# Expert up weights loaded 16 KB per partition, with the token rows written in a permuted column order

## The chip, the cores and the metric

The kernel runs on one core of one Trainium2 chip. The time is the device time of one execution in microseconds (us). The kernel before takes 1584.23 us, the median of 3 runs (1581.51 to 1584.6).

## What is computed

One layer of a streaming encoder, for 1024 frames of a new stream and 64 frames of a running one; everything is float32. The projection, the two kinds of attention and the output product come first; the change touches the mixture of experts behind them:

```python
x = x + moe(rms_norm(x, g_ffn))          # x: 1088 tokens of 1024 columns

def moe(xf):
    # 4 groups of 8 experts: the best group of each token, in it the best 2 experts
    expert, gate = hier_route(xf)        # g_logits = xf @ w_group, e_logits = xf @ w_erouter
    for each token t and each of its 2 experts e:
        h = silu(xf[t] @ w1[e]) * (xf[t] @ w3[e])    # w1, w3: 1024 x 512
        out[t] += gate * (h @ w2[e])                 # w2: 512 x 1024
```

There are 32 experts. w1, w3 and w2 of one are 2 MB (2048 KB) each.

## The kernel before, in words

The program writes out one instruction stream for each engine, with semaphores between them: SP issues the plain DMAs, GpSimd (POOL) the indirect ones, PE multiplies, DVE and ACT empty its banks. The order is fixed by hand.

**First stages.** SP loads constants, the first rows of x and w_in (1024 rows of 1960 columns, one DMA, L516; each row of 7840 B is one contiguous piece). Nine tiles of projections follow, then the attention stage, which goes over nine tiles of 128 tokens. A hand-written table (`filler`, L147) says which pieces of other work stand between the eight heads of a tile. Among them, for the tile before the current one: `o0` and `o1` (the output product, added to xres), `xnorm` (L1632 to L1634: DVE writes the normed row xn = xres x rs_x x g_ffn), `xna` and `xnb` (eight transposes of 128 columns of xn on PE, L786 to L789), `lg` (router logits, L790 to L796: eight matmuls, chunk k of the transposed row against `w_route[:, k, :]`). SP stores xn to the DRAM tensor `xn_rows` (L586). The pT copies (L495 and L498) and the row maxima (L1661, L1662) of the attention heads stand on DVE too; ACT takes the exponentials (L1159).

`w_route` is loaded once (L544), behind `w_out`, as `(k p) n -> p k n`: partition p gets rows p, 128 + p, 256 + p and so on, eight pieces of 144 B. PE, ACT and DVE wait for six loads on `wout_in` at tile 0 (L868, L1193, L1742): w_out, w_route, chunk_mask, g_mh, g_ffn and state_c.

**Routing.** From about 909 to 944 us DVE works out which token goes to which slot; meanwhile SP loads the weights of expert 0 and w1 of expert 1 (L602, L603), and after the first two gathers have landed w3 and w2 of expert 1.

**The expert stage.** Each expert takes one block of up to 96 tokens. `load_expert` (L470) issues w1, w3 and w2, one DMA each, by `load_part` (L481 to L483), into one of two buffers each. A load of expert e + 2 waits until PE is through with the same matrix of expert e: w1 for h1_full, w3 for h3_full, w2 for y_full. `load_part` has the form `(k p) n -> p k n` for all three: partition p gets rows p, 128 + p, ..., so w1 and w3 arrive as eight pieces of 2 KB per partition (1024 pieces), w2 as four of 4 KB (512 pieces). PE's order per expert b is hidden_1 (the product with w1, L916), the down-projection of b - 1 (L940), the transposes of the token rows of b + 1 (L907), hidden_3 (the product with w3, L916). In `up` (L911), `w[:, k, ...]` meets `x[:, k, :]`, where chunk k of x is the transpose of columns 128 k to 128 k + 127 of the gathered row: row i of the weights must meet column i of the token row.

GpSimd gathers 96 token rows of 4 KB from `xn_rows` for expert b + 2 (L1343), and adds the result rows of expert b to y (L1354, a scatter that waits for the previous one). Its order is gather, then scatter, in a loop; in time the gather of b + 2 follows the scatter of b - 1 (L1362 to L1366). In the records a float32 matmul counts as two instructions. If an expert had more than 96 tokens, further blocks would follow (L961 to L968); in this run none do.

Of the kernel before, what the change touches and what calls it, by code (L numbers as in the profile page):

```python
# [24 lines left out]
ALU = mybir.AluOpType  # L25
# [3 lines left out]
P = 128  # L29
D = 1024  # L30
KD = D // P
# [143 lines left out]
def build(nc, T, O):  # L175

    ctx = ExitStack()
    with ctx:
# [3 lines left out]
        def sem(name):  # L182
            return ctx.enter_context(nc.semaphore(name))
# [74 lines left out]
        w_route = A(KD, NG + NE)  # L258
# [25 lines left out]
        g_ffn = A(D)  # L284
        xres = A(D)
        xn = A(D)
# [25 lines left out]
        def tiny(n, parts=P):  # L312
            a = small[0:parts, sp[0]:sp[0] + n]
            sp[0] += n
            assert sp[0] <= 512
            return a
# [22 lines left out]
        rs_x = tiny(1)  # L339
# [26 lines left out]
        gate_in, mixw_in, wout_in = sem("gate_rows_in"), sem("mix_weights_in"), sem("w_out_in")  # L366
# [29 lines left out]
        x1_sq, x1_rs, xn_ok = sem("res_squares"), sem("res_rstd"), sem("xn_ready")  # L396
# [17 lines left out]
        def wait_full(eng, key):  # L414

            b, k = fills[key]
            eng.wait_ge(full[b], k + 1)
            return bank(RB[b])

        def wait_read(eng, key):  # L420

            b, k = fills[key]
            eng.wait_ge(read[b], k + 1)

        def done_read(ins, key):
            ins.then_inc(read[fills[key][0]], 1)
# [11 lines left out]
        def bc(ap, shape):  # L438
            return ap.unsqueeze(len(ap.shape)).to_broadcast(shape)
# [30 lines left out]
        def load_expert(eng, e, s, signals, done=None):  # L470

            row_up, row_down = ahead(eng, e * D), ahead(eng, e * FF)
            count = None if done is None else ahead(eng, done)
            for row, dst, src, signal, used in ((row_up, w1s[s], "w1", signals[0], h1_full),
                                                (row_up, w3s[s], "w3", signals[1], h3_full),
                                                (row_down, w2s[s], "w2", signals[2], y_full)):
                if done is not None:
                    eng.wait_ge(used, count)
                load_part(eng, row, dst, src, signal)

        def load_part(eng, row, dst, src, signal):  # L481
            rows = T[src].rearrange("e a n -> (e a) n")[bass.ds(row, T[src].shape[1]), :]
            eng.dma_start(dst, rows.rearrange("(k p) n -> p k n", p=P)).then_inc(signal, 16)  # L483

        def gate_col(b):
            return slot_gate[:, bass.ds(b, 1)]
# [21 lines left out]
        def _(sp_):  # L508
# [32 lines left out]
            sp_.dma_start(g_ckv, T["g_ckv"].to_broadcast([P, KL])).then_inc(wuq_in, 16)  # L541
            sp_.dma_start(z_rec, z_dram[0:P, Z_MQ:]).then_inc(zr_in, 16)
            sp_.dma_start(w_out, T["w_out"].rearrange("(k p) n -> p k n", p=P)).then_inc(wout_in, 16)
            sp_.dma_start(w_route, T["w_route"].rearrange("(k p) n -> p k n", p=P)).then_inc(wout_in, 16)  # L544
            for n in range(-1, NT + 1):
                if n >= 1:

# [4 lines left out]
                if n + 1 < NT:  # L552

                    r = slice((n + 1) * P, (n + 2) * P)
                    src = cn[(NC + n + 1) % 2]
# [45 lines left out]
            wait_read(sp_, ("lg", NT - 1))  # L601
            load_expert(sp_, 0, 0, (w1_in[0], w3_in[0], w2_in[0]))  # L602
            load_part(sp_, D, w1s[1], "w1", w1_in[1])  # L603

            for s in range(2):
# [777 lines left out]
        def _(dve):  # L1383
            link = chain(dve, dve_link)
            TT, TS, STT = dve.tensor_tensor, dve.tensor_scalar, dve.scalar_tensor_tensor
# [134 lines left out]
            def fill_work(key):  # L1520
                what, n = key
# [47 lines left out]
                elif what == "qkm":  # L1569
                    o = wait_full(dve, key)  # L1570
                    dve.wait_ge(e_ok, n + 1)
                    done_read(TT(Dm, Dm, o.rearrange("p (a b) -> p a b", b=P), ALU.mult), key)
                elif what in ("ua", "ub"):

                    o = wait_full(dve, key)
                    cur, nxt = state[n % 2], state[(n + 1) % 2]
                    h0 = 0 if what == "ua" else 2
                    if n:
                        wait_read(dve, ("ub", n - 1))
                    if n == 1:  # L1580
                        dve.wait_ge(state_out, 16)

                    mid = cur if n else nxt
                    for h in range(h0, h0 + 2):
                        u = o[:, (h - h0) * CAUG:(h - h0 + 1) * CAUG]
                        dec = decb[0:DK, h * NCH + 2 * n:h * NCH + 2 * n + 1]
                        STT(mid[DK:P, h], cur[0:DK, h], dec, u[0:DK], ALU.mult, ALU.add).then_inc(st1_ok, 1)
                    dve.wait_ge(st1_ok, HM * n + h0 + 2)
                    for h in range(h0, h0 + 2):
                        u = o[:, (h - h0) * CAUG:(h - h0 + 1) * CAUG]  # L1590
                        dec = decb[DK:P, h * NCH + 2 * n + 1:h * NCH + 2 * n + 2]
                        ins = STT(nxt[0:DK, h], cur[DK:P, h], dec, u[DK:P], ALU.mult, ALU.add)
                    done_read(ins, key)
                elif what in ("ia", "ib"):
                    o = wait_full(dve, key)
                    h0 = 0 if what == "ia" else 2
                    view = o[:, 0:2 * CAUG].rearrange("p (a b) -> p a b", b=CAUG)
                    if what == "ia" and n:
                        dve.wait_ge(h_ok, n)
                    done_read(TT(num[:, h0:h0 + 2], view, bc(gt[:, 32 + h0:34 + h0], [P, 2, CAUG]), ALU.mult), key)  # L1600
                    wait_read(dve, key)
                elif what in ("na", "nb"):
                    o = wait_full(dve, key)
                    h0 = 0 if what == "na" else 2
                    view = o[:, 0:2 * CAUG].rearrange("p (a b) -> p a b", b=CAUG)
                    done_read(TT(num[:, h0:h0 + 2], num[:, h0:h0 + 2], view, ALU.add), key)
                    if what == "nb":
                        mlstm_ratio(n)
                elif what == "hsq":
                    dve.wait_ge(hsq_ok, n + 1)  # L1610
                    dve.tensor_reduce(st_m, Dm, AX, ALU.add).then_inc(hs_ok, 1)
                    dve.wait_ge(og_ok, n + 1)
                    link(STT(og, og, 1.0, g_mh, ALU.add, ALU.mult))
                elif what == "hout":

                    dve.wait_ge(hr_ok, n + 1)
                    link(TT(hm, hm, bc(rs_m, [P, HM, DV]), ALU.mult))
                    if n:
                        wait_full(dve, ("mxb", n - 1))
                    STT(mix[:, BANK:], hm.rearrange("p a b -> p (a b)"), 0.5, og, ALU.mult,  # L1620
                        ALU.mult).then_inc(mm_ok, 1)
                elif what == "mxb":
                    o = wait_full(dve, key)
                    if n:
                        wait_full(dve, ("lg", n - 1))
                    done_read(dve.tensor_copy(mixT[:, 4:8], o.rearrange("p (a b) -> p a b", b=P)), key)
                elif what in ("o0", "o1"):
                    o = wait_full(dve, key)
                    dve.wait_ge(xres_in, 16 * (n + 1))
                    lo = 0 if what == "o0" else BANK  # L1630
                    done_read(TT(xres[:, lo:lo + BANK], xres[:, lo:lo + BANK], o, ALU.add), key)
                elif what == "xnorm":  # L1632
                    dve.wait_ge(x1_rs, n + 1)
                    STT(xn, xres, rs_x, g_ffn, ALU.mult, ALU.mult).then_inc(xn_ok, 1)  # L1634
                elif what == "xnb":
                    o = wait_full(dve, key)
                    wait_full(dve, ("o1", n))
                    done_read(dve.tensor_copy(xnT[:, 4:8], o.rearrange("p (a b) -> p a b", b=P)), key)
                elif what == "lg":
                    o = wait_full(dve, key)  # L1640
                    done_read(TT(logits[:, n], o[:, 0:NG + NE], b_route, ALU.add), key)

            def mlstm_ratio(n):

                wait_read(dve, ("na", n))
                wait_read(dve, ("nb", n))
                link(STT(den[:, 0:HM], num[:, :, DV], -1.0, num[:, :, DV], ALU.mult, ALU.max))
                link(TT(den[:, 0:HM], den[:, 0:HM], gt[:, 96:96 + HM], ALU.max))
                link(dve.reciprocal(den[:, HM:], den[:, 0:HM]))
                if n:  # L1650
                    dve.wait_ge(mm_ok, n)
                TT(hm, num[:, :, 0:DV], bc(den[:, HM:], [P, HM, DV]), ALU.mult).then_inc(h_ok, 1)
# [81 lines left out]
            for n in range(-1, NT + 1):  # L1734
# [27 lines left out]
                for key in filler(n, HA):  # L1762
                    fill_work(key)
# [166 lines left out]
```

## Time and profile before

| | before |
|---|---|
| median of 3 runs | 1584.23 us |
| the profiled execution, own time | 1581.9 us |
| its span | 1580.1 us |
| mean granted TensorE clock | 0.947 |
| PE busy | 1438.2 us, 91% |
| DVE, ACT, POOL busy | 483.0, 296.6, 203.8 us |
| DMA | 277.63 MB in 110091 packets, mean 176 GB/s |

PE is TensorE's matmul, PEld its weight load, SPq the queue of SP. The page gives busy shares, then the span in 40 equal slices (39.5 us each), where a 9 is 90% or more. "DMA share" is the mean busy share of the core's 16 DMA engines; overlapping packets can bring it above 1. A packet is one contiguous piece. In brackets behind a group of instructions stands the engine's idle time before it and what released it.

### The profile page before, as it was taken

What the parts mean: (1) busy time and instruction counts of PE and PEld (TensorE: products, weight loads), DVE (VectorE), ACT (ScalarE), POOL (GpSimd) and SP (SyncE); (2) the same over time, 40 slices, a digit from 0 to 9 for tenths busy, and PEclk for the clock granted to TensorE, in tenths of its full rate; (3) what the DMA queues carried; (4) which work ended last, traced back from release to release, by engine and by line L of the source; (5) the groups of instructions that cost most, each with busy time, mean ns of one, the idle gap of its engine ahead of it and who ended that gap; (6) DMA issues with size and microseconds to landing.
All of it is one profiled execution on the core that took longest, in us unless ns stands there. A gap on an engine that the chain in (4) does not pass through costs nothing. (4 is left out here: it accounts for less than half of the span.)

```text
span 1580.1 us, 29898 instructions
## 1 busy us (share of the span) xinstructions
PE 1438.2 (91%) x12716; PEld 985.3 (62%) x12716; DVE 483.0 (31%) x1002; ACT 296.6 (19%) x634; POOL 203.8 (13%) x291
## 2 busy tenths in 40 slices
PE   5899999659998999999999838999999999999996
PEld 2444444236667667768677427777777777777773
DVE  3100100266456557647455461111111111111110
ACT  5201010133323233334332100000000001000000
POOL 3100000022022112101020001111111111111110
PEclk9999999868978999999999859999999999999998
DMA  7021211421011101101101068999999999999992
GB/s 274 14 78 39 77 39 51 145 73 45 24 52 61 68 22 47 68 21 48 60 3 41 27 219 285 356 363 358 362 365 357 363 360 366 370 358 354 361 365 87
DMA packets 110091, 277.63 MB, mean 176 GB/s; under 512 B 8952, under 2 KB 12920, under 8 KB 110028
## 3 DMA queue, kind: packets, MB, share of 16 engines
q1 hardware_dynamic: 102864, 255.33, 44.7%
q0 software_dynamic: 7168, 21.51, 5.4%
q8 instruction: 38, 0.62, 0.2%
q14 instruction: 21, 0.17, 0.0%
HBM read 248.40 MB, written 32.05 MB: 177 GB/s over the span
## 5 line engine op out<-in xcount | busy, mean ns | idle before, releaser
L916 PE MATMUL psum<-arena 128*64 128x96 f32 x8192 | 355.6, 246 | 14.4 <-DMA arena<-in_w 11.6
L916 PEld LDWEIGHTS psum<-arena 128*64 128x64 f32 x8192 | 345.6, 136 | 22.8 <-issue 18.6
L689 PE MATMUL psum<-arena 128*128 128x512 f32 (+1 forms) x576 | 238.1, 574 | 0.6 <-DVE arena L1424 0.6
L940 PE MATMUL psum<-arena 128*96 128x512 f32 x512 | 227.5, 596 | 0.8 <-issue 0.8
L689 PEld LDWEIGHTS psum<-arena 128*128 128x128 f32 x576 | 108.8, 190 | 124.2 <-issue 124.2
L940 PEld LDWEIGHTS psum<-arena 128*96 128x96 f32 x512 | 80.6, 162 | 124.2 <-issue 120.5
L784 PE MATMUL psum<-arena 128*128 128x512 f32 x288 | 130.4, 607 | 0.8 <-issue 0.8
L643 PE MATMUL psum<-ident,arena 128*128 128x128 f32 (+1 forms) x468 | 76.0, 312 | 59.0 <-DVE arena L1518 27.1
L846 PE MATMUL psum<-arena 128*128 128x64 f32 (+3 forms) x848 | 110.1, 274 | 1.5 <-DVE arena L498 0.8
L643 PEld LDWEIGHTS psum<-ident,arena 128*128 128x128 f32 (+1 forms) x468 | 62.2, 155 | 78.8 <-DVE arena L1518 28.8
L846 PEld LDWEIGHTS psum<-arena 128*128 128x128 f32 (+3 forms) x848 | 101.7, 189 | 8.8 <-issue 1.8
L816 PE MATMUL psum<-arena 96*128 96x512 f32 (+4 forms) x224 | 100.1, 561 | 0.4 <-DVE small L1500 0.4
L1159 ACT ACTIVATE arena<-psum,small 64x1104 f32<-64x1104 f32 (+8 forms) x72 | 57.7, 802 | 207.8 <-DVE small L1662 207.8
L784 PEld LDWEIGHTS psum<-arena 128*128 128x128 f32 x288 | 54.4, 194 | 63.6 <-issue 62.4
L1833 DVE COPY arena<-psum 128x768 f32<-128x768 f32 x32 | 30.7, 959 | 203.9 <-PE psum L907 203.9
L1252 POOL TENSOR_SCALAR small<-small 128x2 f32<-128x2 f32 (+4 forms) x44 | 14.4, 328 | 578.6 <-ACT arena L1079 189.8
L1212 ACT ACTIVATE arena<-psum 128x384 f32<-128x384 f32 x32 | 15.7, 492 | 380.4 <-PE psum L916 338.6
L1434 DVE TENSOR_SCALAR arena<-psum,small 128x512 f32<-128x512 f32 x18 | 13.5, 751 | 219.6 <-PE psum L689 219.6
L1218 ACT ACTIVATE arena<-psum,slot_gate 96x1024 f32<-96x1024 f32 x32 | 35.6, 1112 | 217.9 <-PE psum L940 217.9
L1839 DVE SCALAR_TENSOR_TENSOR arena<-arena,psum 128x384 f32<-128x384 f32 x32 | 17.8, 555 | 184.8 <-ACT arena L1212 184.8
L829 PE MATMUL psum<-ident,arena 128*128 128x128 f32 (+3 forms) x424 | 63.0, 288 | 9.6 <-ACT arena L1133 3.8
L1350 POOL COPY now_out<-slot_out 128x1 uint32 (+1 forms) x32 | 5.9, 183 | 478.7 <-ACT arena L1218 478.7
(218 smaller groups left out, 1303.9 us busy)
## 6 DMA issues: line engine op xcount, KB each, us to landing
arena<-in_w SPq DMA_DIRECT2D x96, 2048.0 KB, 20.0
arena<-in_x_rows SPq DMA_DIRECT2D x18, 512.0 KB, 5.2
z_rows<-arena SPq DMA_DIRECT2D x9, 980.0 KB, 4.5
arena<-in_w_in SPq DMA_DIRECT2D x1, 7840.0 KB, 23.2
arena<-z_rows SPq DMA_DIRECT2D x9, 768.0 KB, 5.2
out_y<-arena SPq DMA_DIRECT2D x9, 512.0 KB, 2.6
xn_rows<-arena SPq DMA_DIRECT2D x9, 512.0 KB, 2.9
arena<-in_w_out SPq DMA_DIRECT2D x1, 4096.0 KB, 17.1
```

What stands on the lines that cost most here:

```text
L643: ins = pe.transpose(o[0:width, i * P:i * P + rows], src, ident[0:rows, 0:rows])
L689: ins = pe.matmul(o[:, 0:hi - lo], xT[s][:, k, :], w_in[:, k, lo:hi], start=(k == 0), stop=(k == KD - 1))
L784: ins = pe.matmul(o, mixT[:, k, :], w_out[:, k, lo:lo + BANK], start=(k == 0), stop=(k == KD - 1))
L816: pe.matmul(o[0:q, lo:hi], qT[n % 2][:, h, 0:q], KT[:, h, k0:k0 + hi - lo], start=True, stop=True)
L829: ins = pe.transpose(o[0:w, i * P:i * P + q], probs[0:q, lo:lo + w], ident[0:q, 0:q])
L846: ins = pe.matmul(o, pT[0:w, i, 0:q], v, start=(i == 0), stop=(i == len(blocks) - 1))
L916: ins = pe.matmul(o[c:c + CT, j * EB:(j + 1) * EB], w[:, k, j * P + c:j * P + c + CT], x[:, k, :], start=(k == 0), stop=(k == KD - 1))
L940: ins = pe.matmul(bank(5 + c)[0:EB], hT[:, k * EB:(k + 1) * EB], w2s[s][:, k, c * BANK:(c + 1) * BANK], start=(k == 0), stop=(k == KF - 1))
L1159: act.activation(probs[0:q, 0:w], bank(0, 3)[0:q, 0:w], ACT.Exp, bias=nmax[0:q, h:h + 1], accum_out=rsum[0:q, h:h + 1]).then_inc(s_read, 1)
L1218: act.activation(ye[s][0:EB], bank(5, 2)[0:EB], ACT.Copy, scale=gate_col(col)[0:EB]).then_inc(y_read, 1)
L1833: dve.tensor_copy(xeT[s], bank(0, 2).rearrange("p (k t) -> p k t", t=P)[:, :, 0:EB]).then_inc(xeT_read, 1)
L1839: STT(uu, th, 1.0, bank(2)[:, 0:KF * EB], ALU.add, ALU.mult).then_inc(u_ok, 1)
```

## The change

Three edits. `load_part` takes the form `(p k) n -> p k n` for w1 and w3: partition p gets rows 8 p to 8 p + 7, which adjoin in DRAM, 16 KB. w2 keeps its form. `w_route` gets the same form, 1152 B per partition. With that, chunk k of the weights holds rows k, 8 + k, 16 + k, ...; so the token row must have column 8 q + k at place 128 k + q, and the norm writes it so: its output is viewed with q outside and k, in steps of 128 elements, inside, while xres and g_ffn are read in their own order. xn, `xn_rows`, the transposes and the gathered rows all carry the permuted order; nothing else uses them.

```diff
         def load_part(eng, row, dst, src, signal):
             rows = T[src].rearrange("e a n -> (e a) n")[bass.ds(row, T[src].shape[1]), :]
-            eng.dma_start(dst, rows.rearrange("(k p) n -> p k n", p=P)).then_inc(signal, 16)
+            form = "(k p) n -> p k n" if src == "w2" else "(p k) n -> p k n"
+            eng.dma_start(dst, rows.rearrange(form, p=P)).then_inc(signal, 16)
...
-            sp_.dma_start(w_route, T["w_route"].rearrange("(k p) n -> p k n", p=P)).then_inc(wout_in, 16)
+            sp_.dma_start(w_route, T["w_route"].rearrange("(p k) n -> p k n", p=P)).then_inc(wout_in, 16)
...
                 elif what == "xnorm":
                     dve.wait_ge(x1_rs, n + 1)
-                    STT(xn, xres, rs_x, g_ffn, ALU.mult, ALU.mult).then_inc(xn_ok, 1)
+                    by_row = lambda a: a.rearrange("p (q k) -> p q k", k=KD)
+                    STT(xn.rearrange("p (k q) -> p q k", k=KD), by_row(xres), rs_x, by_row(g_ffn), ALU.mult,
+                        ALU.mult).then_inc(xn_ok, 1)
```

## Rows read from the trace of the kernel before

**Rows 1.** The page: the span in 40 slices.

```profile
DMA  7021211421011101101101068999999999999992
```

**Rows 2.** Table of stages, 10 to 1546 us.

```profile
core 0: us, PE busy (x) PEld busy (x) DVE busy (x) ACT busy (x) POOL busy (x), PEclk, DMA share, GB/s
10.00:25.00 15.00, 10.52 (x34) 4.90 (x32) 5.75 (x13) 9.60 (x25) 6.32 (x7) 1.00 1.01 426
920.00:935.00 15.00, 0.61 (x3) 0.33 (x1) 12.73 (x45) 0.00 (x0) 0.00 (x0) 0.50 1.04 397
960.00:1140.00 180.00, 178.19 (x2761) 136.66 (x2762) 20.69 (x30) 14.89 (x19) 25.50 (x36) 1.00 1.01 352
1141.00:1546.00 405.00, 393.42 (x5883) 295.07 (x5880) 43.45 (x63) 33.70 (x42) 58.08 (x82) 1.00 1.03 362
```

**Rows 3.** Waits of PE, 960 us to the end (us in total, times, longest).

```profile
PE psum L916 <- DMA arena<-in_w: 11.6, 18, 1.1
```

**Rows 4.** Timeline of PE, expert stage: start us, us, what, idle before.

```profile
973.92 7.11 PE L940 MATMUL psum<-arena 128*96 128x512 f32 x16
...
992.45 7.11 PE L940 MATMUL psum<-arena 128*96 128x512 f32 x16
...
1141.10 7.11 PE L940 MATMUL psum<-arena 128*96 128x512 f32 x16
...
1155.21 5.55 PE L916 MATMUL psum<-arena 128*64 128x96 f32 x128 [0.83 <-DMA arena<-in_w]
...
1546.21 7.11 PE L940 MATMUL psum<-arena 128*96 128x512 f32 x16
```

**Rows 5.** DMA, 10 to 25, then 920 to 935, then 1141 to 1546 us.

```profile
DMA packets 815, 6.39 MB, mean 426 GB/s; under 512 B 0, under 2 KB 0, under 8 KB 815
...
DMA packets 2445, 5.96 MB, mean 397 GB/s; under 512 B 48, under 2 KB 48, under 8 KB 2445
...
q0 software_dynamic: 4600, 13.67, 13.2%
```

**Rows 6.** DMA of the whole span: a queue (MB, share), issues (us to landing).

```profile
q8 instruction: 38, 0.62, 0.2%
...
arena<-in_w SPq DMA_DIRECT2D x96, 2048.0 KB, 20.0
...
arena<-in_w_route SPq DMA_DIRECT2D x1, 144.0 KB, 18.5
```

**Rows 7.** Groups of DVE by shape: busy us, mean ns.

```profile
L1634 DVE SCALAR_TENSOR_TENSOR arena<-arena,small 128x1024 f32<-128x1024 f32 x9 | 11.6, 1285 | 2.5 <-POOL small L1254 2.2
...
L1476 DVE TENSOR_TENSOR_SCAN arena<-arena 4x1152 f32<-4x1152 f32 x1 | 2.5, 2545 | 0.0
...
L1477 DVE COPY small<-arena 4x18 f32<-4x18 f32 x1 | 0.2, 165 | 0.0
L1483 DVE COPY small<-small 4x16 f32<-4x16 f32 x1 | 0.2, 163 | 0.0
```

**Rows 8.** Timeline around the norm: the eighth tile, then the last.

```profile
855.43 0.11 DVE L1661 MEMSET psum<- 64x64 f32 x1 [0.16 <-PE psum L818]
...
856.85 1.13 ACT L1159 ACTIVATE arena<-psum,small 128x1040 f32<-128x1040 f32 x1 [2.83 <-DVE small L1662]
...
858.36 0.87 PE L829 MATMUL psum<-ident,arena 128*128 128x128 f32 x6
...
906.50 1.97 PE L643 MATMUL psum<-ident,arena 128*128 128x128 f32 x8 [4.27 <-DVE arena L1634]
```

**Rows 9.** Timeline near 1110 us, then landings of the gather (min/median/max).

```profile
1111.35 10.90 PE L916 MATMUL psum<-arena 128*64 128x96 f32 x256
...
1115.65 1.00 POOL L1343 DMA_INDIRECT arena<-xn_rows,now_tok  x1 [0.83 <-POOL now_tok L1340]
...
1129.13 0.82 PE L907 MATMUL psum<-ident,arena 96*128 96x96 f32 x8
...
DMA to landing us min/median/max: 4.2/8.5/9.9
```

## The prediction

> **What bounds the kernel now.** The page comes first. Its slices show the DMA engines lightly used up to slice 23 and at nine tenths from slice 25 on [rows 1]. That stretch is the expert stage, from about 950 us to the end. The table of stages says both are full there: between 1141 and 1546 us PE works 393.4 of 405 us, the DMA share is 1.03, at 362 GB/s [rows 2]. So I need the row that says which of them yields. The list of waits has one entry in which PE waits for a transfer: L916, the up-projections, on the expert weights, 18 times, 11.6 us [rows 3]. The timeline of PE gives the period. Down-projections (L940) start at 973.92 and 992.45, 18.53 us apart, with nothing idle between; between 1141.10 and 1546.21 lie 21 periods of 19.29 us, and the gaps stand where w1 of the next expert is due [rows 4]. I read it so: PE needs 18.53 us per expert, the DMA engines 19.29. Double buffers give the loads a lead of some experts, which is used up by about 1140 us; from there the loads set the pace. From 973.92 to 1546.21 there are 30 periods: 572.29 us, against 30 x 18.53 = 555.9 us if PE never waited. The difference, 16.4 us, is all that faster loads can give (11.6 us of named waits, the rest late restarts after them). In front of the stage no load of an expert is waited for, and behind it stand one scatter and the end.
>
> **What the change does to the loads.** w1 and w3 of each expert, 64 of the 96 expert loads, go from 1024 pieces of 2 KB to 128 pieces of 16 KB; w2 stays at 512 of 4 KB. Bytes and destination addresses in SBUF are as before. What a piece costs beside its bytes comes from two stretches with nothing else on the DMA engines: 10 to 25 us (w_in, pieces of 7840 B) moved 815 packets, and 920 to 935 us (2 KB and 4 KB pieces) 2445 packets, 48 of them tiny, of 5.96 MB [rows 5]. Per engine that is 15 x 16 / 815 = 0.2945 us for 7840 B and 15 x 16 / 2397 = 0.1001 us for 2486 B on the average. The line through both has 36.3 ns per 1000 B and 9.8 ns per piece. Eight pieces of 2 KB made one save 7 x 9.8 = 69 ns; each engine has 16 such pieces per expert (2 tensors x 128 / 16), so 1.10 us per expert, an estimate that extrapolates from 7840 to 16384 B. The ends: with the rate of the 7840 B pieces alone, 4.19 MB at 426 instead of 397 GB/s [rows 2] save 0.72 us. On the other side the page's instruction queue moved 38 packets of 16 KB in 0.2% of 16 engines' span, or 1.3 us each instead of the 0.60 us of my line [rows 6]; these come singly, each with its way to memory and back, and mine come in a row as w_in's do, so I take 1.10 us and keep that end for a rival.
>
> How much is enough? Without waits the 30 periods need 16.4 us less, and the DMA engines are full from the start of them, so 16.4 / 30 = 0.55 us per expert suffices. 1.10 us is twice that and the 0.72 us still more than that: I expect PE to set the whole stage, and the gain to be 16.4 us, cut off by PE at 18.53 us per expert. What is late next is PE itself; loads will land with a growing lead.
>
> **The token rows.** The norm (L1634) writes element (q, k) to column k x 128 + q, so its output steps 512 B from element to element; it reads as before. The transposes, the gather and the matmuls keep their addresses, so PE's instructions keep number and shape. L1634 takes 1285 ns, nine times. The trace has no strided write of this size. A strided read of 18 elements 256 B apart takes 165 ns beside 163 ns for 16 adjoining ones: nothing to speak of. The slowest row per element is the scan, 2545 ns for 1152, or 2.2 ns each, which would make the norm 2.26 us [rows 7]. I take nothing (nearest row) and keep plus 1.0 us as the other end. What hides it: in the eighth tile the norm stands two copies ahead of the row maximum on DVE; that starts 0.16 us after PE's scores, and the exponential behind it ends near 858.0 where PE takes it up at 858.36. So of 1.0 us more 1.0 - 0.16 - 0.38, some 0.5, would reach PE in each of eight tiles, and all of it in the last tile, where PE's transposes wait for the norm until 906.50: 8 x 0.5 + 1.0 = 5.0 us [rows 8].
>
> The Trainium skill (Advanced Engine Details and Errata, Memory Cachelines) speaks against this write: accesses that each fall into another 16-byte line of SBUF pay a penalty, which it does not price; no row here shows such a write.
>
> **w_route.** One load of 144 KB in 128 pieces instead of 1024. It lands 18.5 us after its issue, behind w_out [rows 6], and PE and the others wait not for it but for six loads, of which state_c is issued last. At most 56 x 9.8 ns = 0.5 us, off the path: nothing. SP's instructions are the same in number.
>
> **The gather.** GpSimd's indirect DMAs share the 16 engines with the loads. The gather issued at 1115.65 lands after 8.5 us (9.9 at most), and the transposes that need it start at 1129.13, 13.5 us after the issue [rows 9]; 5 us are spare. If its rows take turns with the loads' packets, a row now waits behind 0.60 us instead of 0.08. Some ten rows per engine (13.67 MB in 21 periods [rows 5], scatter and gather) make at most 10 x 0.52 = 5.2 us more. Only w3's eight packets per engine lie in the queue at that time, though (its product ends at about 1117, w1's at 1122), so 8 x 0.52 = 4.2 us: just inside. I put its cost at nothing, with a rival.
>
> **The sum.** 1581.9 us of the profiled execution less 16.4 is 1565.5. That execution stands 2.3 us under the median of the runs, 1584.23; I carry the difference over: 1567.8, say 1568.
>
> **The rivals.**
> 1. The loads get faster, but by less than 0.55 us per expert; the gain is 30 x the saving. With 0.36 us, half of the lower end, it is 10.8 us: 1573. For it: fixed costs may overlap while two queues are served. Against: even the rate measured at 7840 B is enough. Chance 0.10. 
> 2. Nothing happens, because the memory gives no more than the 360 GB/s of the expert stage whatever the pieces: 1584. Against it are the 426 GB/s of 10 to 25 us and 397 GB/s of 920 to 935 us [rows 2]; for it, that no row has so large pieces beside gathers. Chance 0.06. The Trainium skill (DMA: Bandwidth & Descriptors, Specifications) puts the memory's limit per core at about 358 GB/s, by which this rival would be the forecast; the trace's 426 does not agree.
> 3. Slower: the gather lands late. Its place is PE's L907, the decision point a landing 13.5 us after issue instead of 8.5. It would take two 16 KB packets ahead of each row instead of one. With a landing at 14.5 us PE waits 1 us in 30 experts: 1568 + 30 = 1598. Chance 0.06.
> 4. Slower: a 16 KB packet costs 1.3 us in a row as well [rows 6]. Then w1 and w3 alone take 16 x 1.3 = 21 us per expert instead of 10.8, and 30 x 10 us are added: about 1880. For it is one rounded row, against it that 7840 B pieces run at 426 GB/s. Chance 0.02.
> 5. The gain comes, but the norm's strided write costs 1.0 us each: 1568 + 5.0 = 1573. Chance 0.12; half of that cost is as likely as all of it.
>
> The forecast itself has 0.64. Together the cases that end under 1581 hold 0.86, rival 2 holds 0.06, the slower ones 0.08. A measurement of this kernel tells about 0.2% (3.2 us) from no change. The range: PE's 18.53 us leaves no room for a larger gain, so only the scatter of runs (3.1 us) lies below: 1564. Above, it takes in rivals 1 and 5 with both costs at part: 1576. Left out are rivals 2 to 4 and some of the tails.
>
> **What would show it.** In the changed profile: about 51,900 DMA packets rather than 110,091 (64 loads x 896 fewer, and 896 for w_route); no PE wait on in_w, or a few below 1 us; L940 every 18.53 us up to the end of the stage; a DMA share in the late stage below the 1.03 of now, and GB/s up from 362 to some 375, since the same bytes pass in less time; in_w landings well under 20 us; L1634 near 1285 ns. I am wrong if L940 stays above 18.6 us with in_w as the releaser (rivals 1, 2, 4), if PE waits at L907 for xn_rows (rival 3), or if L1634 is above 1.5 us and PE idles in the attention stage (rival 5).

## The result, and the profile after

The changed kernel takes 1598.19 us, the median of 20 runs (1582.9 to 1635.33); the kernel before, run beside it, 1584.22 us (20 runs, 1579.4 to 1609.43). The ratio is 1.0067, 95% interval 1.0042 to 1.0092: slower by 0.7%, where 1568 us was forecast. The ratio leaves the disturbed runs out (5 of the 20 of the changed kernel) and is worth 10.6 us; the medians take in all runs and differ by 14.0. The profiled execution took 1590.24 us, with a span of 1588.3.

The table of stages, the waits of PE for transfers in the expert stage, and the DMA of 1141 to 1546 us, of the changed kernel, answer to [rows 2], [rows 3] and [rows 5]:

```profile
core 0: us, PE busy (x) PEld busy (x) DVE busy (x) ACT busy (x) POOL busy (x), PEclk, DMA share, GB/s
10.00:25.00 15.00, 9.77 (x36) 4.72 (x35) 6.45 (x14) 9.60 (x25) 7.19 (x8) 1.00 1.01 426
960.00:1140.00 180.00, 170.35 (x2630) 132.05 (x2632) 19.48 (x28) 13.31 (x17) 23.79 (x34) 0.98 0.95 340
1141.00:1546.00 405.00, 400.44 (x5962) 299.31 (x5962) 44.95 (x65) 34.99 (x44) 59.99 (x86) 1.00 1.01 366
```

```profile
PE psum L908 <- DMA arena<-xn_rows,now_tok: 11.4, 8, 2.6
```

```profile
DMA packets 22033, 148.21 MB, mean 366 GB/s; under 512 B 2286, under 2 KB 2286, under 8 KB 16555
...
arena<-in_w SPq DMA_DIRECT2D x64, 2048.0 KB, 19.9
...
arena<-xn_rows,now_tok POOLq DMA_INDIRECT x21, 13.3
```

No product waits for its weights any more. In their place PE's transposes wait eight times for the gathered token rows, 11.4 us in all, about as much as before in another place: the gather lands a median of 13.3 us after its issue instead of 8.5. The timeline of PE and GpSimd shows one such wait, and the line's landings (min/median/max) answer to [rows 9]:

```profile
996.41 1.01 POOL L1344 DMA_INDIRECT arena<-xn_rows,now_tok  x1 [0.82 <-POOL now_tok L1341]
...
1003.00 7.11 PE L941 MATMUL psum<-arena 128*96 128x512 f32 x16
...
1012.71 0.88 PE L908 MATMUL psum<-ident,arena 96*128 96x96 f32 x8 [2.61 <-DMA arena<-xn_rows,now_tok]
...
DMA to landing us min/median/max: 4.2/13.3/16.3
```

The gather is issued at 996.41, its rows would be wanted at 1010.1, when the down-projection ends, and come at 1012.7.

The other new thing is in front of the expert stage. First the norm by shape [rows 7], then its last place on DVE and the first and last down-projection on PE [rows 8, 4]:

```profile
L1636 DVE SCALAR_TENSOR_TENSOR arena<-arena,small 128x1024 f32<-128x1024 f32 x9 | 17.9, 1993 | 2.5 <-POOL small L1255 2.2
```

```profile
913.52 1.96 DVE L1636 SCALAR_TENSOR_TENSOR arena<-arena,small 128x1024 f32<-128x1024 f32 x1 [2.20 <-POOL small L1255]
...
984.21 7.11 PE L941 MATMUL psum<-arena 128*96 128x512 f32 x16
...
1554.40 7.11 PE L941 MATMUL psum<-arena 128*96 128x512 f32 x16
```

The norm takes 1.99 us instead of 1.28. The span is 8.2 us longer, and this is where: the last norm starts 8.4 us later (913.52 against 905.16); from there to the first down-projection it is 70.7 us instead of 68.8, 1.9 more; the 30 periods take 570.2 us instead of 572.3, 2.1 less; the rest is 33.9 us in both. The profiled execution thus shows 8 us, where the ratio is worth 10.6 and the medians differ by 14.

### The profile page after: what moved, and what is told of

Same layout as the page of the kernel before. It is cut to its first block and busy times, and to the rows that moved or that the text cites. A ratio compares the mean times of both kernels' runs of the same rounds, so it can differ in the third digit from the quotient of the medians.

```text
span 1588.3 us, 29898 instructions
## 1 busy us (share of the span) xinstructions
PE 1443.4 (91%) x12716; PEld 989.6 (62%) x12716; DVE 489.4 (31%) x1002; ACT 296.2 (19%) x634; POOL 203.4 (13%) x291
## 2 busy tenths in 40 slices
DMA packets 51851, 277.63 MB, mean 175 GB/s; under 512 B 7928, under 2 KB 12024, under 8 KB 43596
## 5 line engine op out<-in xcount | busy, mean ns | idle before, releaser
L785 PE MATMUL psum<-arena 128*128 128x512 f32 x288 | 134.0, 621 | 0.8 <-issue 0.8
L1435 DVE TENSOR_SCALAR arena<-psum,small 128x512 f32<-128x512 f32 x18 | 13.5, 751 | 219.2 <-PE psum L690 219.2
```

Of the source, the lines that this page charges most:

```text
L785: ins = pe.matmul(o, mixT[:, k, :], w_out[:, k, lo:lo + BANK], start=(k == 0), stop=(k == KD - 1))
```

## The experiments

Each ran in five rounds beside the kernel before, whose median was 1583.2 to 1587.1 us in these four sessions. The sessions were on three chips, so experiments of different sessions are compared by their ratios to the kernel before. By the way: in the expectations, "568 + the norm's 8" means 1568.

**e1, the loads alone.** Only the edit of `load_part`; the norm and w_route are left in their old order.

> The 16 KB pieces for w1 and w3 alone; the norm writes xn in its own order and w_route keeps its form, so the up-products meet columns in another order than the rows (routing and all sizes are as before). Theory A (the loads gain about 16 us, and the gather of the token rows, landing 13.3 us after issue instead of 8.5, gives most of it back; the strided norm costs some 8 us besides): between 1584 and 1592 us, PE waits on xn_rows of 10 us or more, no wait on in_w, L1634 at 1285 ns. Theory B (the strided norm is the whole loss): 1568 us, gather waits as a side effect gone or below 3 us. Theory C (the DMA engines are still full with 16 KB pieces, the gather waits are only where that shows): as A, with the DMA share at 1.0 or more.

Measured: 1585.57 us, ratio 1.0009 (0.9976 to 1.0043); 8.4 us of waits on xn_rows in 6 places, none on in_w; gather landings 13.0 us. The 30 periods take 569.0 us. So the 16 KB pieces alone gain nothing that these runs can tell (their interval is 0.3% to each side), and the norm is not the whole loss: theory B falls, A or C stands.

**e2, the norm alone.** Only the edits of w_route and of the norm; the loads are left in their old order.

> The permuted norm and w_route alone; w1 and w3 load in 2 KB pieces as before, so the up-products meet columns in another order than the rows (routing and all sizes are as before). Theory A: plus 6 to 9 us, 1590 to 1593, the norm at 1990 ns nine times, the last norm about 6 to 8 us later than before, and the expert stage as before with 11 us of waits on in_w, none on xn_rows. Theory B: plus 20 us or more, 1604. Theory C: as A.

Measured: 1603.42 us, ratio 1.0106 (1.0062 to 1.0149). The expert stage is as before (573.9 us for 30 periods, 13.4 us of waits on in_w), the last norm starts at 926.22. Nearer to B's number than to A's: the norm costs twice what A had for it, 17 us by the ratio. The losses of e1 and e2 add up to 1.15%, more than the 0.67% of the changed kernel, but their intervals (0.6% to 1.7% for the sum) reach down to it.

**e3 and e4, an earlier gather that was none.** I meant to issue the gather one expert earlier, and wrote the loop as scatter of b, then gather of b + 3:

```diff
-                    pool.wait_ge(xeT_full, b + 1)
-                    gather(s, b + 2, xe_in[s])
                     scatter(s, b, ye_out[s], ye_out[1 - s], 16 * (j + s))
+                    pool.wait_ge(xeT_full, b + 2)
+                    gather(1 - s, b + 3, xe_in[1 - s])
```

> The changed kernel whole, with GpSimd issuing the gather of expert b + 3 behind the scatter of b, one expert earlier than now. Theory A: no PE wait on xn_rows and none on in_w, L941 every 18.53 us, 1574 to 1578 us (568 + the norm's 8), the runs closer together than the 50 us they spread now. Theory B: 1594 or more, since the gather was no cause. Theory C: waits on in_w take the place of those on xn_rows, period near 19 us, 1586 to 1592.

> The kernel before with the same earlier gather and nothing else. All theories: the time of before within 2 us, 11 us of waits on in_w as before, since its gathers were never late; if it is faster by 5 us or more, hidden gather waits were part of the time before too, and theory A credits the 16 KB pieces with too much.

Measured: 1600.77 us, ratio 1.007 (1.0023 to 1.0118), and 1586.29 us, ratio 1.0031 (0.9995 to 1.0067). That order is the one the loop had all along, since the gather of b + 2 stands at the head of the next turn, behind the scatter of b - 1. The two are repeats of the changed kernel and of the kernel before, and agree with them.

**e5, the changed kernel with the gather truly earlier.** The buffer of b + 4 is free once the rows of b + 2 are transposed, right behind the down-projection that the scatter of b waits for:

```diff
+            for s in range(2):
+                pool.wait_ge(xeT_full, s + 1)
+                gather(s, 2 + s, xe_in[s])
...
-                    pool.wait_ge(xeT_full, b + 1)
-                    gather(s, b + 2, xe_in[s])
                     scatter(s, b, ye_out[s], ye_out[1 - s], 16 * (j + s))
+                    pool.wait_ge(xeT_full, b + 3)
+                    gather(s, b + 4, xe_in[s])
```

> The changed kernel whole, with the gather of expert b + 4 behind the scatter of b, where the buffer has just come free: truly one expert earlier. (In e3 and e4 it was not: GpSimd's loop already issued the gather of b + 3 behind the scatter of b, so those two repeat the changed kernel and the kernel before.) Theory A (late gathers give back what the loads gain): no wait on xn_rows and none on in_w, L941 every 18.53 us, about 13 us under the changed kernel: 1585. Theory C (the DMA engines are full with 16 KB pieces too): the waits move to in_w, period 19.0 us, time of the changed kernel within 4 us.

Measured: 1584.81 us, ratio 0.9989 (0.9955 to 1.0023). The stage of e5 in the table of stages, cut at 1512 us since its last load is issued at 1525.7 us and has landed by 1541.3, and the landings of its gathers:

```profile
1141.00:1512.00 371.00, 371.00 (x5609) 280.40 (x5607) 41.38 (x60) 32.05 (x40) 56.17 (x79) 1.00 1.01 373
1512.00:1546.00 34.00, 34.00 (x501) 24.83 (x498) 3.18 (x5) 3.20 (x4) 1.79 (x3) 1.00 0.73 281
```

```profile
DMA to landing us min/median/max: 4.1/13.0/16.1
```

The gathers land as late as ever after their issue, but PE works all 405 us and waits for no transfer. The 30 periods take 556.2 us, 18.54 each. A's 13 us are there (12 by the two ratios, 1.0067 and 0.9989). C falls as a cause: the DMA engines are still full while the loads last, with a share of 1.01 at 373 GB/s, but PE doesn't wait for them.

**e6, the loads alone with the earlier gather.** e1 with the loop of e5.

> The 16 KB pieces for w1 and w3 alone (norm and w_route as before, so the up-products meet columns in another order), with the gather of b + 4 behind the scatter of b. e1 without the earlier gather took 1585.6 us, 13 us of it over PE's 18.53 us per expert. Theory A: 1572 us, no waits of PE on transfers in the expert stage. Theory C: 1583 or more, with waits on in_w.

Measured: 1569.48 us (6 runs), ratio 0.9884 (0.9838 to 0.9929). This is the time that was forecast for the change, and what the loads are worth when the gather is early and the norm plain. PE waits for no transfer. The stage of e6, whose last load has landed by 1535.3 us:

```profile
1141.00:1512.00 371.00, 371.00 (x5610) 280.36 (x5608) 41.32 (x60) 32.08 (x40) 55.18 (x78) 1.00 1.01 374
1512.00:1546.00 34.00, 33.24 (x440) 22.92 (x437) 3.18 (x5) 3.21 (x4) 3.21 (x4) 1.00 0.60 221
```

**e7, strided read in place of the strided write.**

```diff
-                    by_row = lambda a: a.rearrange("p (q k) -> p q k", k=KD)
-                    STT(xn.rearrange("p (k q) -> p q k", k=KD), by_row(xres), rs_x, by_row(g_ffn), ALU.mult,
+                    by_row = lambda a: a.rearrange("p (q k) -> p k q", k=KD)
+                    STT(xn.rearrange("p (k q) -> p k q", k=KD), by_row(xres), rs_x, by_row(g_ffn), ALU.mult,
```

> The changed kernel with the same permuted norm, but written in order and read with steps of 32 B. Theory D (the norm's longer write delays PE in the attention stage, and with PE's idle moments comes more time at half clock): if L1636 falls to 1285 ns, the stage ends as before, near 907 us, and the time is that of e1, 1586 us, 12 to 15 under the changed kernel. If strided reads cost the same as strided writes, L1636 stays near 2.0 us and the time at 1598. Rival E (the longer norm is hidden; the spread of the attention stage is chance): 1598 whatever L1636 takes.

Measured: 1595.26 us, ratio 1.0064 (1.0032 to 1.0096). The norm takes 2072 ns: reading in steps of 32 B is no better than writing in steps of 512 B. It doesn't tell D from E.

**e8, e7 with the gather of e5.**

> Both amendments: norm with strided read, gather of b + 4 behind the scatter of b. Theories A and D: 1572 us, faster than both kernels. Theory C: 1585. Theory E: as e5.

Measured: 1587.19 us, ratio 0.9994 (0.9966 to 1.0023), 30 periods 557.7 us, no wait for a transfer. The 1572 us of A and D would have needed a short norm; it takes 2073 ns, and the time is that of e5. The 8 us under e7 (11 by the ratios) are again the gathers.

**e9, the permutation in the transposes.** e6, and in `gather_transposes`:

```diff
-                    ins = pe.transpose(bank(0, 2)[:, k * P:k * P + EB], xe[s][0:EB, k * P:(k + 1) * P],
+                    ins = pe.transpose(bank(0, 2)[:, k * P:k * P + EB], xe[s][0:EB].rearrange("t (q k) -> t k q", k=KD)[:, k, :],
                                        ident[0:EB, 0:EB])
```

> 16 KB pieces for w1 and w3, gather of b + 4 behind the scatter of b, norm and w_route as in the kernel before; the permutation is made by the eight transposes of the gathered rows, which read every eighth column (steps of 32 B). Theory A+D (nothing is lost but by late gathers and the longer norm): if the strided transposes cost PE nothing, 1569.5 us as e6, faster than both kernels. If they take twice their 0.1 us each, 0.8 us in 31 experts: 1594. The row of L908 by shape tells which.

Measured: 1577.29 us, ratio 0.9959 (0.9929 to 0.9989). The transposes of e9, then those of e10 with the plain read, in the groups by shape:

```profile
L908 PE MATMUL psum<-ident,arena 96*128 96x96 f32 x256 | 33.4, 274 | 7.6 <-issue 7.6
```

```profile
L907 PE MATMUL psum<-ident,arena 96*128 96x96 f32 x256 | 27.1, 249 | 7.6 <-issue 7.6
```

A strided read costs PE some 0.2 us per expert; the 30 periods take 563.2 us, 7.0 more than in e5 and e6. Between the two answers expected, nearer to the free one. It beats both kernels, the one before by 0.4%.

**e10, the kernel before with the gather of e5.**

> The kernel before with the gather of b + 4 behind the scatter of b, nothing else: the control for e6 and e9. Theory A: its gathers were never late and its loads still are, so 1584 us with 11 us of waits on in_w, within 2 us of the kernel before. Rival F (the earlier gather alone spreads the transfers better and gives the gain of e6 without 16 KB pieces): 1570, in_w waits below 3 us.

Measured: 1585.41 us, ratio 1.0035 (0.9996 to 1.0073), and this wait of PE:

```profile
PE psum L916 <- DMA arena<-in_w: 12.7, 16, 1.4
```

So the earlier gather gives nothing by itself; F falls.

**e11, a longer norm without a stride.**

```diff
-                    STT(xn, xres, rs_x, g_ffn, ALU.mult, ALU.mult).then_inc(xn_ok, 1)
+                    for at in range(0, D, 147):
+                        part = slice(at, min(at + 147, D))
+                        last = STT(xn[:, part], xres[:, part], rs_x, g_ffn[:, part], ALU.mult, ALU.mult)
+                    last.then_inc(xn_ok, 1)
```

> The kernel before with its norm written in seven plain pieces of 147 columns (the last shorter), no stride anywhere, so that DVE spends some 2.0 us on it instead of 1.28. Theory D (what costs is DVE's time at this place, by delaying PE and by the time at half clock that follows, not the strided access as such): as e2, 1595 to 1603, more than 70 us at half clock between 400 us and the last norm. Rival G (the strided access slows other engines' accesses to SBUF): 1584 to 1588, the attention stage as before.

Measured: 1597.91 us, ratio 1.008 (1.0051 to 1.0108). Its norm in the timeline:

```profile
432.54 2.06 DVE L1636 SCALAR_TENSOR_TENSOR arena<-arena,small 128x147 f32<-128x147 f32 x7
```

The same 2 us of DVE cost 13 us by the ratio without any stride (e2: 17, with intervals that overlap). G falls: beyond its length no cost of the strided access shows. The table of stages over the eight tiles, 430 to 905 us, of the kernel before, e6, the changed kernel, e11 and e2, in this order (the last three columns are the granted clock, the DMA share and GB/s):

```profile
430.00:905.00 475.00, 451.13 (x2421) 327.16 (x2421) 278.12 (x612) 150.12 (x361) 67.84 (x93) 0.95 0.12 42
```

```profile
430.00:905.00 475.00, 452.38 (x2410) 328.22 (x2409) 275.89 (x605) 149.99 (x361) 67.30 (x92) 0.94 0.12 42
```

```profile
430.00:905.00 475.00, 451.39 (x2406) 327.89 (x2405) 282.78 (x610) 148.64 (x359) 67.09 (x91) 0.94 0.12 41
```

```profile
430.00:905.00 475.00, 452.28 (x2396) 332.64 (x2396) 277.37 (x638) 149.01 (x359) 67.11 (x91) 0.92 0.12 41
```

```profile
430.00:905.00 475.00, 452.49 (x2378) 333.88 (x2377) 271.31 (x570) 148.97 (x359) 67.11 (x91) 0.91 0.12 41
```

PE is as busy in all five, some 95% of this stretch, but the granted clock is 0.95 and 0.94 with the short norm and 0.94, 0.92 and 0.91 with the long one (unrounded 0.946, 0.939, 0.935, 0.917 and 0.907). From the first norm to the last it takes 473.0 and 475.8 us with the short norm, 481.9, 489.6 and 496.3 with the long one. Where the clock agrees (e4, which is the kernel before over again, and the changed kernel, both 0.935), it is 475.9 against 481.9 us: 6.0 us, and eight norms are 8 x 0.71 = 5.7 us longer. The remaining 8 to 15 us of e11 and e2 over e6 go with 2 to 3 hundredths of the clock, which over 475 us are 10 to 14 us.

In PE's own records the larger part is not waiting. Between the first and the last norm PE stands idle for 24.0 us in the kernel before, 25.6 in e11 and 26.3 in e2, but is busy for 448.9, 464.0 and 470.0 us: the same products take longer, since more of them run at half clock.

**e12, pieces of 4 KB.** Gather order, norm and w_route of the kernel before, and:

```diff
+            if src == "w2":
+                rows = rows.rearrange("(k p) n -> p k n", p=P)
+            else:
+                rows = rows.rearrange("(a p c) n -> p a (c n)", p=P, c=2)
+                dst = dst.rearrange("p (a c) n -> p a (c n)", c=2)
+            eng.dma_start(dst, rows).then_inc(signal, 16)
...
-xe[s][0:EB, k * P:(k + 1) * P]
+xe[s][0:EB].rearrange("t (a q c) -> t a c q", c=2, q=P)[:, k // 2, k % 2, :]
```

> Pieces of 4 KB for w1 and w3 (two adjoining rows per piece), gather order, norm and w_route as before; the transposes read every second column (steps of 8 B). By the 9.8 ns per piece this saves 0.63 us per expert, just over the 0.55 needed. Theory A (the gather lands late because each of its rows waits behind a 16 KB packet): landing near 9 us, no PE wait on xn_rows, waits on in_w below 3 us, 1569 to 1573 us. Rival H (the gather is late with any faster loads): waits on xn_rows of 5 us or more.

Measured: 1574.56 us, ratio 0.9937 (0.9908 to 0.9966): the lowest of all kernels but e6, which leaves the permutation of the rows out. The profiled execution took 1599.86 us; in it the granted clock is 0.88 between 430 and 905 us, in code that is the same as in the kernel before, but 1.00 in the stretch of the expert stage that is read here:

```profile
1141.00:1546.00 405.00, 405.00 (x6122) 311.11 (x6119) 44.16 (x65) 34.12 (x43) 61.76 (x87) 1.00 1.02 368
```

```profile
arena<-in_w SPq DMA_DIRECT2D x64, 2048.0 KB, 17.8
...
arena<-xn_rows,now_tok POOLq DMA_INDIRECT x22, 8.8
```

```profile
L912 PE MATMUL psum<-ident,arena 96*128 96x96 f32 x256 | 35.0, 281 | 7.5 <-issue 7.5
```

The loads are fast enough for PE never to wait for them, and the gather lands after 8.8 us as with pieces of 2 KB: no wait at all, with the old order of gathers. H falls: it is the 16 KB packets that hold up the gather, not faster loads as such. The periods are 18.8 us, for the transposes are slow here too, at 281 ns each.

**e13, e14 and e15, the norm in two places.** The strided norm is cut in two, half at its place, half at the head of the next slot of the hand-written order:

```diff
-        ... ("ub", n)] * now + [("xnorm", n - 1)] * old,
-        4: [("kn", m), ...
+        ... ("ub", n)] * now + [("xnorm0", n - 1)] * old,
+        4: [("xnorm", n - 1)] * old + [("kn", m), ...
...
+                elif what in ("xnorm0", "xnorm"):
+                    dve.wait_ge(x1_rs, n + 1)
+                    q = slice(0, P // 2) if what == "xnorm0" else slice(P // 2, P)
+                    by_row = lambda a: a.rearrange("p (q k) -> p q k", k=KD)[:, q, :]
+                    ins = STT(xn.rearrange("p (k q) -> p q k", k=KD)[:, q, :], by_row(xres), rs_x, by_row(g_ffn),
+                              ALU.mult, ALU.mult)
+                    if what == "xnorm":
+                        ins.then_inc(xn_ok, 1)
```

e14 does it for the permutation of e12, in four instructions of 256 columns.

> The changed kernel with the gather of b + 4 behind the scatter of b, and its strided norm cut into two halves, one at the norm's place (slot 3 of the hand-written order), one at the head of slot 4, each near 1.0 us. Theory I (what costs is the 2.0 us in one piece in front of one row maximum, which PE then waits for and which the clock follows): the attention stage as before, less than 70 us at half clock between 400 us and the last norm, 1570 us, faster than both kernels. Rival J (any more DVE time in the attention stage costs as much, wherever it stands): 1585, as e5.

> Pieces of 4 KB for w1 and w3, gathers and transposes as in the kernel before, the permutation (every second column) made by the norm in four strided instructions, two in slot 3 and two in slot 4, w_route to match. Theory I: 1568 to 1571 us, 7 us under e12 (1574.6), since the transposes read plainly again. Rival J: 1580 or more.

> The permuted norm in two halves and the permuted w_route alone, loads in 2 KB pieces, so the up-products meet columns in another order: e2 with the norm cut. Theory I: 1584 to 1587 us, as the kernel before. Rival J: 1600, as e2 (1603).

Measured: e13 1580.94 us, ratio 0.9968 (0.9935 to 1.0000); e14 1586.72 us, 0.9992 (0.9957 to 1.0027); e15 1591.92 us, 1.0038 (1.0002 to 1.0074). A half takes 1106 ns, the four parts of e14 659 ns each. Against the norm in one piece e15 gains 11 us on e2, e13 4 us on e5, with intervals that touch. None reaches I's number, all but e14 lie below J's. I also wanted less than 70 us at half clock between 400 us and the last norm, and e13 and e15 have 78.5 us each. So cutting the norm in two doesn't free the attention stage of its cost. Whether it lowers it, and by how much the place and the amount count, these runs don't settle. The gathers of e14 land after 8.6 us beside 4 KB pieces, as in e12; its 30 periods take 558.8 us, with two waits on in_w of 0.8 us together, so that 4 KB pieces are just about enough.

## Why the prediction was wrong

- **PE 18.53, loads 19.29 us per expert, at most 16.4 us to gain: right.** e5 and e6 have 30 periods of 18.54 us, 556.2 us in all, and e6 takes 1569.5 us where 1568 was forecast.
- **1.10 us per expert saved by larger pieces: enough, but too large a term.** Packets are 51851, as counted. The waits on in_w are gone in every kernel with pieces of 16 KB. But the loads never run ahead of PE. In e5 and e6 the DMA engines are full up to 1512 us (share 1.01, 373 and 374 GB/s), and from issue to landing a load takes 22.8 and 22.9 us in the median between 1141 and 1546 us, against 20.3 before, where well under 20 was forecast; in e6 the w1 of the seventh expert took 19.7 us, that of the thirtieth 23.6. Moving 374 instead of 362 GB/s takes 0.6 us off a period of 19.29, and the period fell by 0.75, to PE's 18.54. That is near the lower end of the prediction, 0.72, and above the 0.55 that was needed, with little to spare. Rivals 1, 2 and 4 fall all the same.
- **"I put its cost at nothing" (the gather): the first step that failed.** The prediction had 13.5 us as the decision point, had 10 x 0.52 = 5.2 us more as a bound, which is 13.7 us and beyond it, and then argued itself back to 4.2 us with the queue as PE would leave it if the loads ran ahead. But the share stayed at 1.01 and landings of w at 19.9 us: the queue was full, as before, and it is no emptier in e5 and e6, where no gather holds PE up. The gather lands at 13.3 us in the median, 16.3 at most. Rival 3 was the right mechanism with a chance of 0.06. Its price was too high, 30 us against the 14.0 and 12.8 us that the 30 periods lose by it (570.2 against 556.2 in e5, 569.0 in e1 against 556.2 in e6), since a late gather delays PE and so the next one's due time; only 8 of 30 are late enough to be seen.
- **The strided norm at nothing: the second.** It takes 1.99 us. The row it was priced by, a copy of 18 elements on 4 partitions, is almost all fixed cost (18 elements at the norm's 1.25 ns are 23 of its 165 ns) and could not show 0.69 ns more per element; the other end, plus 1.0 us, was the better guide. The Trainium skill (Advanced Engine Details and Errata, Memory Cachelines) had said that accesses which each fall into another 16-byte line are penalised; the trace agrees, with 0.7 us for 1024 elements.
- **"Some 0.5 would reach PE" of 1.0 us: the third, and the dearest.** By that step 0.71 us would cost 8 x 0.17 + 0.71, or 2 us. e2 and e11 measure 17 and 13. At equal clock the delay reaches PE whole, 6.0 us in eight tiles. I had read the slack from the eighth tile, which is the most forgiving: of the eight intervals from norm to norm the last two (70.2 and 52.1 us in e4 and e6) grow by 0.0 and 0.3 us in the changed kernel, the first two (56.2 and 54.5) by 1.3 and 2.5. The same comes out of whole executions: at a mean clock of 0.943 to 0.946 four runs of e5 took 1572.6 to 1576.5 us and four of e6 1566.5 to 1570.4, 6 us apart, and nine norms are 6.4 us longer. But the medians of e5 and e6 are 15 us apart. The other 9 go with the clock, for which the prediction had no term.
- **w_route at nothing: not tested alone.** It changes together with the norm in every run, and no run has it alone.

The two costs that the forecast had at nothing came together: late gathers gave the loads' gain back (e1: ratio 1.0009), the norm came on top (e2), and that makes the changed kernel slower.

That the longer norm lowers the clock is shown by e11, whose only edit it is. Its 12 runs have a mean clock of 0.934 to 0.943, 0.939 in the median; the 34 of the kernel before beside them that the ratio counts have 0.945 in the median, and all but one of them 0.940 or more. The other pairs agree: 0.936 in e5 against 0.946 in e6. By what way a delay of 0.7 us does it is not shown. A single profile says little here: the kernels with 2 us of norm in one place (the changed one, e2, e3, e5, e7, e8, e11) spend 65 to 96 us at half clock between 400 us and the last norm, those with 1.28 us (before, e1, e4, e6, e9, e10) 52 to 65 us; but e12, with the short norm, has 123 us in its profiled execution.

## What to carry to other kernels

Larger pieces made the full DMA engines faster here, and slower for the small transfers that share them: the gather landed 4.8 us later beside 16 KB packets, so look at the slack of the small transfers first, or take the size that is just large enough (4 KB rid PE of its waits with the gathers at their old place, and beat both kernels at 1574.6 us). Price each place where a permutation can be made by what it delays, not by how busy the engine is: on PE, which is full, the strided transposes cost 7 us in all, while 0.7 us per tile on DVE, busy for 31% of the span, cost 13 to 17. Price a strided instruction by a row of its own size, not by a small one. Slack behind an engine has to be read in the tightest tile, and in a stage where PE is nearly full a short delay cost its own length and, through the clock, as much again.

## What was not expected of the hardware

- DVE, float32, 1024 elements: 1285 ns in order, 1993 ns when written in steps of 512 B, 2072 ns when read in steps of 32 B.
- PE's transposes of 128 columns: 249 ns in order, 274 ns when read in steps of 32 B (e9), 281 ns in steps of 8 B (e12). The shorter step helps nothing.
- 0.7 us of DVE work more in nine tiles cost 13 us (e11), about half of it with the granted clock (0.92 against 0.94 to 0.95 in the attention stage).
- The gather's landing follows the packet size of the other queue and not in proportion: 8.5 us beside 2 KB packets, 8.8 beside 4 KB, 13.3 beside 16 KB. The scatters, which share the engines too, went from 8.2 to 8.5 and 10.4 us.
- The DMA engines moved 362 GB/s in the expert stage with 2 KB pieces and 374 with 16 KB (e6), full in both.
